# A hybrid trunk kernel: one more projection unit as three bf16 products, and the tokens' low halves made earlier

## The reference, cut to what matters

```
h_l = rmsnorm(x, norm_mix_g[layer]) * (1 + m_l[1]) + m_l[0]
h_c = rmsnorm(ctx, norm_mix_g[layer]) * (1 + m_c[1]) + m_c[0]
p_l = split_projection(h_l, w_in[layer])        # einsum 'bld,de->ble', float32
p_c = split_projection(h_c, w_in[layer])
a_l, a_c = diff_attention_mixer(p_l[0:3], p_c[0:3], ...)   # 512 + 256 columns used as aqk, av
b_l, b_c = hgrn2_mixer(p_l[3:8], p_c[3:8], ...)            # bq, bi, bff, bfb, bg
c_l, c_c = swa_mixer(p_l[8:11], p_c[8:11], ...)            # windowed ("local") heads: q 256, k 128, v 128
x = x + m_l[2] * (concat(a_l, b_l, c_l) @ w_out[layer])
```

## Time and profile before

| | us |
|---|---|
| median of 3 runs | 1765.88 (1764.0 to 1766.35) |
| the profiled execution | 1764.34 |
| its span | 1762.6 |
| PE busy in it | 1662.9 (94%) |
| DVE busy | 1177.4 (67%) |
| ACT busy | 385.7 (22%) |
| POOL busy | 237.7 (13%) |

### The profile page before, as it was taken

The page is one execution under the profiler, slowest core; times in us unless marked ns, Lnnn a source line. Parts: engine busy times, 40 slices in busy tenths (PEclk is TensorE's granted clock), DMA queues, the critical chain, the costliest instruction groups (busy, mean ns, idle before and its releaser), DMA issues.

```text
span 1762.6 us, 40515 instructions
## 1 busy us (share of the span) xinstructions
PE 1662.9 (94%) x18193; PEld 1151.0 (65%) x18193; DVE 1177.4 (67%) x1278; ACT 385.7 (22%) x713; POOL 237.7 (13%) x108
## 2 busy tenths in 40 slices
PE   6999999899999999999999888999999999999998
PEld 2434557674544444445465565899989889898987
DVE  1344476975443444215477777998989988999897
ACT  1101254453422222112125353010111010101010
POOL 0035100020656430000461010000000000000000
PEclk9999999999999999999999999999999999999999
DMA  9932201014656425231230116999999999999994
GB/s 378 331 144 72 96 1 48 1 49 153 230 191 237 180 108 191 72 96 48 97 120 0 49 76 260 412 419 422 422 421 421 422 422 418 423 404 422 408 421 199
DMA packets 82484, 409.14 MB, mean 232 GB/s; under 512 B 14008, under 2 KB 20856, under 8 KB 51600
## 3 DMA queue, kind: packets, MB, share of 16 engines
q1 hardware_dynamic: 80120, 405.54, 57.6%
q10 hardware_dynamic: 2200, 1.08, 0.3%
HBM read 405.55 MB, written 1.05 MB: 231 GB/s over the span
## 4 chain that ended last, share of the span: by engine, by line
PE 70%; DVE 12%; DMA 10%; issue 4%; ACT 2%; PEld 1%; ACTq 0%; DVEq 0%; SPq 0%; POOL 0%; PEldq 0%; POOLq 0%
PE PS L1669 12%; PE PS L803 10%; DMA ARENA<-in_moe_w 8%; PE PS L1627 6%; PE PS L2047 5%; PE PS L807 5%; PE PS L2024 4%; PE PS L2023 4%; PE PS L2025 4%; PE PS L2043 3%; DVE ARENA L2160 3%; PE PS L1533 2%; PE PS L485 2%; PE PS L1395 2%; DVE ARENA L1008 1%
## 5 line engine op out<-in xcount | busy, mean ns | idle before, releaser
L2160 DVE TENSOR_TENSOR ARENA<-ARENA 128x2816 bf16<-128x2816 f32 (+1 forms) x168 | 525.4, 3151 | 39.7 <-DMA ARENA<-in_moe_w 38.9
L2023 PE MATMUL PS<-ARENA 128*128 128x88 bf16 x2816 | 354.3, 206 | 26.5 <-DVE ARENA L2160 20.1
L2023 PEld LDWEIGHTS PS<-ARENA 128*128 128x128 bf16 x2816 | 341.4, 123 | 36.3 <-DVE ARENA L2160 25.7
L2024 PE MATMUL PS<-ARENA 128*128 128x88 bf16 x2816 | 353.4, 210 | 5.6 <-issue 5.5
L2025 PE MATMUL PS<-ARENA 128*128 128x88 bf16 x2816 | 353.0, 210 | 2.6 <-issue 2.4
L2024 PEld LDWEIGHTS PS<-ARENA 128*128 128x128 bf16 x2816 | 343.5, 125 | 11.9 <-issue 11.9
L2025 PEld LDWEIGHTS PS<-ARENA 128*128 128x128 bf16 x2816 | 313.2, 111 | 3.0 <-issue 2.9
L803 PE MATMUL PS<-ARENA 128*128 128x512 bf16 (+1 forms) x1104 | 227.9, 356 | 0.0
L1669 PE MATMUL PS<-ARENA 128*128 128x512 bf16 x984 | 215.8, 379 | 0.0
L803 PEld LDWEIGHTS PS<-ARENA 128*128 128x128 bf16 x1104 | 104.8, 97 | 106.7 <-issue 16.4
L1669 PEld LDWEIGHTS PS<-ARENA 128*128 128x128 bf16 x984 | 95.0, 98 | 121.0 <-issue 5.4
(11 more groups left out here) (257 smaller groups left out, 1869.0 us busy)
## 6 DMA issues: line engine op xcount, KB each, us to landing
ARENA<-in_moe_w SPq DMA_DIRECT2D x128, 1408.0 KB, 17.7
ARENA<-in_moe_w SPq DMA_DIRECT2D x48, 1536.0 KB, 21.0
ARENA<-in_ada_w SPq DMA_DIRECT2D x24, 2048.0 KB, 10.1
ARENA<-in_ffn_w SPq DMA_DIRECT2D x15, 2048.0 KB, 7.6
ARENA<-in_w_in SPq DMA_DIRECT2D x11, 2048.0 KB, 7.9
ARENA<-in_moe_w SPq DMA_DIRECT2D x16, 1024.0 KB, 19.6
ARENA<-in_w_in SPq DMA_DIRECT2D x6, 1024.0 KB, 6.9
ARENA<-in_w_out SPq DMA_DIRECT2D x8, 512.0 KB, 4.4
```

The lines of the kernel that those rows point to most:

```text
L2023: pe.matmul(out, hi[:, f], HEH[:, k, :], start=k == 0 and b % 5 == 0, stop=False, skip_group_check=True)
L2024: pe.matmul(out, hi[:, f], HEL[:, k, :], start=False, stop=False, skip_group_check=True)
L2160: dve.tensor_tensor(WLO[q % NSLOT][:, 0:n], RAW[q % NSLOT][:, 0:n], WHI[q % NSLOT][:, 0:n], ALU.subtract).then_inc(S("m_lo"), 1)
```

## The change

"c" enters the list HALVED and the table HALVED_IN, in one part. DVE halves its weights after the copy of n = 2, and the tokens' low halves move from behind the copy of n = 3 to ahead of the copy of n = 2, in both layers (behind the setup in layer 0). PE's fp32 matmuls of "c", 64 over both layers, become 192 in bf16, and PE waits for the halved weights ahead of n = 4, where it waited for the load before.

```diff
-        HALVED = ("bff", "bfb", "bq", "av", "bi")
+        HALVED = ("c", "bff", "bfb", "bq", "av", "bi")
...
-        HALVED_IN = {"bff": 1, "bfb": 1, "bq": 1, "av": 1, "bi": 4}
+        HALVED_IN = {"c": 1, "bff": 1, "bfb": 1, "bq": 1, "av": 1, "bi": 4}
...
         def dve_proj_first(dve, L):
             for n in range(2 * NT):
-                if L == 0 and n == 2:
-                    dve_setup(dve)
+                if n == 2:
+                    if L == 0:
+                        dve_setup(dve)
+                    dve_tokens_low(dve, L)
...
                 dve_proj_one(dve, L, n)
-                if n == 3:
-                    dve_tokens_low(dve, L)
+                if n == 2:
+                    dve_proj_halve(dve, L, "c")
                 if n == 5:
                     dve_proj_halve(dve, L, "bff")
```

## The result

| | before | after |
|---|---|---|
| median, lowest to highest (6 runs each, same chip) | 1766.12 (1764.0 to 1766.78) | 1777.66 (1771.63 to 1785.37) |
| the profiled execution | 1764.34 | 1782.85 |
| its span | 1762.6 | 1781.1 |
| granted clock over the span | 0.998 | 0.978 |
| PE busy in it | 1662.9 | 1684.0 |

The change makes the kernel slower: ratio 1.0066, 95% interval 1.0052 to 1.0080. The forecast was 1755.4, faster. Over the six runs the time follows the granted clock: 1771.63 us at 0.985, 1782.85 at 0.978.

The account below looks back on a forecast made before the run. PE itself was taken to bound both stages of "c" through its fp32 matmuls. Gains of 6.05 us in layer 0 and 4.4 in layer 1, together 10.5, gave 1755.4 us against the median, range 1752.5 to 1759.5.

Parts of the forecast that it names:

- PE's bf16 tile of "c": Layer 0, n = 4 and 5: a tile of 24 bf16 matmuls takes 5.44 us where the fp32 tile costs 7.07.
- no wait at n = 4: DVE's halved weights of "c" are ready before PE comes: slack 1.6 us in layer 0, 1.0 us in layer 1.
- DVE's nine and a half us a layer: Tokens 4.42 us and halving 5.03 us on DVE per layer, covered by slack, so they cost nothing.
- the wait of 2.4 us ahead of spread step 1: Layer 0, after n = 5: PE waits for DVE's line 534 copy 2.4 us instead of 1.46.
- layer 1's 4.4 us: Layer 1, copy of n = 3 to copy of n = 7: 16.2 us instead of 20.64, a gain of 4.4.
- the first expert load behind the output projection: The expert stage's first load waits for an output projection matmul (14.7 us, line 1533), so its stream moves up whole.
- The gain of layer 0: Layer 0's "c" stage on PE: n = 8 starts at 101.7 us instead of 107.75, a gain of 6.05.
- the 10.5 us: Gain of both layers' "c" stages together, expected to reach the kernel's end: 1755.4 us against the median.
- The lock on the port pair: Skill's exclusive VectorE lock against GpSimd: new halvings could hold up GpSimd, but it is idle then, so cost nothing.
- None of the four: Rivals: late halves (1759 us, 0.10), gain swallowed behind (1765.9, 0.07), slower through DVE (1774, 0.04), routing shift (0.01).
- The slower case: Rival: PE waits for DVE's tokens and halving in both layers, 19 us against PE's 10.5; 1774 us, chance 0.04.
- The routing: Rival: different rounding gives an expert more than 88 tokens, eight more expert steps, hundreds of us; chance 0.01.

Follow-up runs that it names:

- e11: Changed kernel plus 48 matmuls of 16 columns ahead of the 17th tile of layer 0's projections; 1756.28 us, ratio 0.9945.
- e10: Kernel before plus 64 matmuls of 16 columns ahead of the 17th tile of layer 0's projections; 1765.79 us.
- e9: Kernel before plus 40 one-column POOL writes ahead of its halving of "bg" in layer 0; 1788.07 us, ratio 1.0119.
- e5: Changed kernel with PE's two waits in layer 0's attention filled by 2 and 6 matmuls of 448 columns; 1756.30 us, ratio 0.9936.
- e12: e3 plus 48 matmuls of 16 columns ahead of the 17th tile of layer 0's projections; 1753.09 us, ratio 0.9926.
- e7: Kernel before plus 13 tiny POOL memsets ahead of its halving of "bg" in layer 0; 1766.40 us.
- e3: Changed kernel with layer 0's halving of "bff" moved behind DVE's first spread copy; 1773.66 us, ratio 1.0038.
- e4: Changed kernel with matmuls filling PE's waits: ten ahead of spread step 1, two and six in layer 0's attention; 1757.68 us, ratio 0.9939.
- e6: Changed kernel with the "bff" move of e3 and the attention filling of e5; 1752.32 us, ratio 0.9931.
- e8: Changed kernel with POOL's halving of "bg" in layer 0 as eight operations of 512 elements instead of four; 1773.42 us.
- e2: The change in layer 0 alone, layer 1 as in the kernel before; 1781.98 us, ratio 1.0086.

## Why the prediction was wrong

**What held.** PE's bf16 tile of "c" (5.52 us against 5.44), no wait at n = 4 in either layer, DVE's nine and a half us a layer at no cost, the wait of 2.4 us ahead of spread step 1 (2.21), layer 1's 4.4 us (4.39 from n = 3 to n = 7), the first expert load behind the output projection (still a wait of 14.8 us). The gain of layer 0 is there too when the clock holds: in e11 n = 8 starts at 102.07, forecast 101.7.

**What failed.** "After n = 7 the heads' norms, GpSimd's rotations and the loads all start from events that move up with PE. ... I expect the 10.5 us to reach the end." They do start from such events, and layer 0's attention starts 2.4 us earlier; but not all that they meet moves with them. A packet of instructions doesn't: it moves when PE gets more instructions (by 10.6 us for 64 short matmuls, e10), and the change gives PE more. It came 1.9 us earlier against the attention and fell into the middle of the load of "bg" (which landed after 9.2 us, not 7.8), POOL's halving came 1.4 us later against PE, DVE's combine and scaling were held up by it (0.51 to 2.01 and 0.17 to 1.14 us), PE waited 1.78 us instead of 0.64, and PE's clock fell to 1.2 GHz for 58 us: +24.7 us where the sum had nothing. e9 shows the links from POOL to the clock in the kernel before, e5 the last one (the wait), e11 and e12 the first ones in the changed kernel, by removal.

**A second miss, smaller: the price of the first wait.** The 2.4 us wait ahead of spread step 1 was priced as a wait alone. In the profiled execution it was 2.21 us, the clock fell there for 6.8 us, and that cost 3.4 us more. But this fall doesn't come with the longer wait alone. In the traces of e7, e9 and e10, which run this part as the kernel before does, PE waited 1.39 to 1.46 us, and the clock fell there as well, for 3.4, 3.4 and 6.8 us; in e11 it waited 2.25 us, and the clock held. Of ten traces with a wait of 1.4 to 2.3 us seven have the fall; of the four where the wait was filled or taken away (e3, e4, e6, e12) none has. So the kernel before pays this price too in some executions, and the one that I read wasn't one of them: a row from a single execution hid it.

**The lock on the port pair.** The prediction cited the Trainium skill ("SBUF — State Buffer", section SBUF: two separate sides, on the shared port pair) and asked whether the new halvings of DVE hold up GpSimd. In layer 0, where POOL starts nothing between 45 and 114 us, they can't. The damage came in the other direction: GpSimd's old halving held up DVE, at 207.75, since it had shifted by 1.4 us. I looked for collisions of the instructions added, not of the old ones that would meet anew.

**The rivals.** None of the four was it. The slower case had the right size by chance (1774) with the wrong mechanism: at n = 4, where that case has it, PE never waited for DVE. The routing didn't shift: PE has 64 matmul records more than before (18257 against 18193), the change's own. The chance of this case was set at 0.04, and that of a slower kernel at 0.05, from that mechanism and the routing alone.

**Open.** How long a wait of PE makes the clock fall. In the attention, waits of 0.64 to 0.92 us mostly go with a clock that holds (of 25 runs of before beside e5 to e8 one was at 1792.08 and clock 0.981, of e7's ten one), with 0.21 + 1.35 us it fell (e3), and eight of e8's ten runs have the time and the clock of a fall, with waits that no trace shows. By what the packet's place is counted also isn't settled: 64 short matmuls moved it by 10.6 us, the change by 1.9. That the packet itself delays the load rests on fourteen traces and on its removal in e11 and e12, not on a packet put there alone.

## What to carry to other kernels

Before a gain upstream is carried to the end, list what runs on its own clock (loads of weights, packets of instructions, another engine's old work) and what it will newly lie beside; where PE works in small tiles with waits of half a microsecond, one microsecond more can cost twenty by the clock. Read PEclk in windows first when a faster stage makes a slower kernel. The cure is cheap: move the late halving or load, or give PE something to do in the wait, and test which by adding the disturbance to the kernel before.

## What the runs showed of the hardware

- A fall of the granted clock outlasts the wait that it goes with: it begins within the wait of 1.35 us (after, e9) or 2.0 to 2.4 us behind it (e3, e2), and the stretches at 0.50 lasted 44 us (e2, e3) to 58 us (after, e9), though in the changed kernel PE was busy in 50.00 of 50.00 us of it.
- The same code and the same wait don't always bring a fall: ahead of spread step 1 the clock held with a wait of 1.46 us (before) and fell with 1.46 (e7); it fell with 2.21 (after) and held with 2.25 (e11).
- PE's wait, not its load, went with the fall: filling the waits with more matmuls (e5) kept 1.00.
- One 16 KB packet of the queue of instructions in the middle of a 2048 KB load went with a landing after 8.9 to 9.4 us (the changed kernel, e2 to e6, e8), against 7.8 to 8.0 in the seven kernels where it stood at the end or outside; in the changed kernel the load has a tail of 1.3 us at 25 GB/s, a sixteenth of its rate.
- A DVE operation of 256 columns with two SBUF inputs that started near the beginning of a subtraction on POOL (1.9 us each) took 1.77 to 2.23 us, and 0.51 where it started 0.23 us ahead of the end of one. The Trainium skill ("SBUF — State Buffer", section SBUF: two separate sides) calls the port pair that the two engines share an exclusive lock. The rows agree: in all thirteen traces in which POOL has four subtractions, the DVE operation ends 0.27 to 0.28 us after the third of them, however early it started.
- Sixteen-column bf16 matmuls took 0.027 us each (64 in 1.75 us), 13 writes of POOL 0.48 us.
